# A hybrid encoder layer on one Trainium2 core: the row roots of the first norm reach all partitions by a store to DRAM and a broadcast load

## The reference

```
def rms_norm(x, g):
    y = xf * lax.rsqrt(jnp.mean(xf * xf, axis=-1, keepdims=True) + EPS)
    return (y * g)
h = rms_norm(x, mix_norm_g[l])
proj = h @ w_in[l]
u_a, v_a, q, k, v = jnp.split(proj, splits, axis=-1)
```

## Time and profile before

| what | value |
|---|---|
| median of 3 runs | 918.72 us (918.25 to 919.39) |
| the profiled execution | 919.09 us |
| its span | 917.3 us |
| PE busy | 909.7 us, 99% of the span |
| ACT, POOL, DVE busy | 429.6, 390.4, 588.9 us |
| granted TensorE clock | 0.999 of full speed |
| chain that ended last | PE 98%, issue 1% |

### The profile page before, as it was taken

The page is one execution under the profiler, slowest core; times in us unless marked ns, Lnnn a source line. Parts: engine busy times, 40 slices in busy tenths (PEclk is TensorE's granted clock), DMA queues, the critical chain, the costliest instruction groups (busy, mean ns, idle before and its releaser), DMA issues.

```text
span 917.3 us, 11969 instructions
## 1 busy us (share of the span) xinstructions
PE 909.7 (99%) x4229; PEld 750.0 (82%) x4229; DVE 588.9 (64%) x785; ACT 429.6 (47%) x835; POOL 390.4 (43%) x387
## 2 busy tenths in 40 slices
PE   9999999999999999999999999999999999999997
PEld 7888888787878888888888888888888888888885
DVE  5759879986779787464453653736547676544754
ACT  6747547856556543243333333333334454444451
POOL 1559732331244379557485574855754000000021
PEclk9999999999999999999999999999999999999999
DMA  9797453211242372744727437264366996656543
GB/s 330 235 267 232 115 161 105 80 70 70 92 138 88 97 220 69 232 136 134 228 68 233 138 126 227 76 226 146 121 223 248 372 368 192 201 187 203 185 138 138
DMA packets 151487, 158.56 MB, mean 173 GB/s; under 512 B 27576, under 2 KB 109060, under 8 KB 151428
## 3 DMA queue, kind: packets, MB, share of 16 engines
q1 hardware_dynamic: 150756, 157.40, 53.0%
q10 hardware_dynamic: 672, 0.40, 0.1%
HBM read 117.26 MB, written 40.50 MB: 172 GB/s over the span
## 4 chain that ended last, share of the span: by engine, by line
PE 98%; issue 1%; ACT 0%; POOL 0%; DVE 0%; POOLq 0%; ACTq 0%
PE ps L859 31%; PE ps L861 31%; PE ps L860 31%; PE ps L1031 1%; PE ps L1054 1%; PE ps L1043 1%; PE ps L979 1%; PE ps L1125 1%; PE ps L883 0%; PE ps L892 0%; PE ps L895 0%; PE ps L898 0%; PE ps L1000 0%; PE ps L990 0%; PE ps L1061 0%
## 5 line engine op out<-in xcount | busy, mean ns | idle before, releaser
L2116 DVE TENSOR_TENSOR P_lo<-P_raw,P_hi 128x512 fp32r<-128x512 f32 x132 | 119.5, 921 | 83.2 <-ACT P_hi L1554 78.8
L859 PE MATMUL ps<-T_hi,P_hi 128*128 128x512 f32 x352 | 136.9, 389 | 0.0
L860 PE MATMUL ps<-T_lo,P_hi 128*128 128x512 f32 x352 | 136.9, 389 | 0.0
L861 PE MATMUL ps<-T_hi,P_lo 128*128 128x512 f32 x352 | 136.9, 389 | 0.0
L801 POOL TENSOR_TENSOR wd<-wd 128x256 f32<-128x256 f32 x88 | 80.9, 919 | 93.6 <-DMA wd<-in_w_down 88.4
L859 PE MATMUL ps<-rb_hi,ra_hi 128*128 128x512 f32 x308 | 119.8, 389 | 0.0
L860 PE MATMUL ps<-rb_lo,ra_hi 128*128 128x512 f32 x308 | 119.8, 389 | 0.0
L861 PE MATMUL ps<-rb_hi,ra_lo 128*128 128x512 f32 x308 | 119.8, 389 | 0.0
L1668 ACT ACTIVATE ra_hi<-ra 128x512 fp32r<-128x512 f32 x77 | 48.6, 631 | 98.8 <-DMA rb<-w_down_T 61.0
L649 POOL TENSOR_SCALAR late<-late 128x1 f32<-128x1 f32 x12 | 6.0, 503 | 191.7 <-ACT junk L1736 178.1
L2225 DVE TENSOR_TENSOR ra_lo<-ra,ra_hi 128x512 fp32r<-128x512 f32 x77 | 55.7, 723 | 36.4 <-ACT ra_hi L1668 36.0
(11 more groups left out here) (286 smaller groups left out, 2018.0 us busy)
## 6 DMA issues: line engine op xcount, KB each, us to landing
wd<-in_w_down SPq DMA_DIRECT2D x44, 256.0 KB, 3.3
w_down_T<-wd SPq DMA_DIRECT2D x22, 512.0 KB, 5.0
ra<-act_S SPq DMA_DIRECT2D x44, 256.0 KB, 2.7
rb<-w_down_T SPq DMA_DIRECT2D x44, 256.0 KB, 3.0
act_S<-Q SPq DMA_DIRECT2D x33, 256.0 KB, 3.7
ra<-act_A SPq DMA_DIRECT2D x33, 256.0 KB, 4.4
rb<-in_w_down SPq DMA_DIRECT2D x33, 256.0 KB, 5.0
P_raw<-in_w_gate SPq DMA_DIRECT2D x22, 256.0 KB, 3.7
```

The source lines that it names most:

```text
L859: mm(dst, lhs[0], rhs[0], start=start, stop=False, skip_group_check=onto)
L860: mm(dst, lhs[0], rhs[1], start=False, stop=False, skip_group_check=onto)
L861: return mm(dst, lhs[1], rhs[0], start=False, stop=stop, skip_group_check=onto)
L2116: tt(w_l[p, m][:], src[:], w_h[p, m][:].bitcast(F32), ALU.subtract).then_inc(w_split, 1)
```

## The change

PE's eight transposes and ACT's two copies go. SP stores the roots as they lie (4 columns of 128 partitions) to a DRAM tensor in row order, two DMAs of 512 single elements each, waits for both, and loads each half back as one row of 512 broadcast to 128 partitions. `x_roots(1)` moves on POOL from behind the last bias copy to behind the 22nd of 29 (`ROOTS1_AT`), since SP now waits for it ahead of the bias wait. `evict` waits for both loads. Product P1_2 and P1_3, which waited for the copies because of their PSUM banks, now wait for the v_a results that lay there.

```
+    root_dram = nc.dram_tensor("row_roots", [T, P], F32, kind="Internal")
...
             for i in range(4):
                 in_block(wA_raw[i], i, 0, 0, slot_in[i])
+            for h in range(2):
+                sp.wait_ge(x_rstd, h + 1)
+                sp.dma_start(root_dram.ap()[HT * h:HT * h + HT].rearrange("t p -> p t"), rstd_x[:, HT * h:HT * h + HT], allow_slow_non_contiguous=True).then_inc(roots_out, 16)
+            sp.wait_ge(roots_out, 32)
+            for h in range(2):
+                sp.dma_start(roots[h][:], root_dram.ap()[HT * h:HT * h + HT].rearrange("t p -> (t p)").partition_broadcast(P)).then_inc(roots_in, 16)
             sp.wait_ge(bias_out, 16)
...
+            ROOTS1_AT = 3 * len(runs) // 4
...
+                if n == ROOTS1_AT:
+                    x_roots(1)
             last.then_inc(rel_built, 1)
-            x_roots(1)
...
-            def roots_T(h):
-                pe.wait_ge(x_rstd, h + 1)
-                pe.wait_ge(v_ready, HT * h + 3 + h)
-                for t in range(HT):
-                    r = HT * h + t
-                    last = nc.tensor.transpose(ps[:, ROOT_BANK[h], t * P:(t + 1) * P], rstd_x[:, r:r + 1].to_broadcast([P, P]), ident[:])
-                last.then_inc(rstd_T, 1)
...
-                    roots_T(0)
...
-                        pe.wait_ge(roots_ready, i - 1)
+                        pe.wait_ge(v_ready, (3, T)[i - 2])
...
-                if j == 0:
-                    roots_T(1)
...
-            def roots_copy(h):
-                act_e.wait_ge(rstd_T, h + 1)
-                if h:
-                    act_e.wait_ge(setup_T, 1)
-                actv(roots[h][:], ps[:, ROOT_BANK[h], :], ACT.Copy).then_inc(roots_ready, 1)
-
-            roots_copy(0)
...
-            roots_copy(1)
...
-                dve.wait_ge(roots_ready, half + 1)
+                dve.wait_ge(roots_in, 32)
```

More of the change, by code:

```diff
@@ L297, in hybrid_trunk_layer @@
     WARM = 15
-    ROOT_BANK, MIX_BANK = (2, 7), (3, 4)
+    MIX_BANK = (3, 4)
     STORES = [[slice(0, D)]] * (T - 1) + [[slice(0, C), slice(C, D)]]
@@ L317, in hybrid_trunk_layer @@
         x_in = [sem(f"x_in{s}") for s in range(4)]
-        x_sq, x_mse, x_rstd, rstd_T, roots_ready, hT0_hi_ready, hT_hi_ready, hT_ready = (
-            sem(n) for n in ("x_sq", "x_mse", "x_rstd", "rstd_T", "roots_ready", "hT0_hi_ready", "hT_hi_ready", "hT_ready"))
+        x_sq, x_mse, x_rstd, roots_out, roots_in, hT0_hi_ready, hT_hi_ready, hT_ready = (
+            sem(n) for n in ("x_sq", "x_mse", "x_rstd", "roots_out", "roots_in", "hT0_hi_ready", "hT_hi_ready", "hT_ready"))
         block_in = [sem(f"block_in{k}") for k in range(K)]
```

## The result

| | before | after |
|---|---|---|
| median of the runs, us | 918.49 (4 runs, 917.96 to 919.39) | 928.84 (4 runs, 928.03 to 929.79) |
| profiled execution, us | 919.09 | 929.79 |
| its span, us | 917.3 | 928.0 |
| mean granted clock of TensorE | 0.999 | 0.993 |

The ratio is 1.0111, with an interval of 1.0099 to 1.0123: the kernel is slower by 10.3 us, where +1.2 was forecast. 928.84 lies outside the range of 918.2 to 922.6, and beyond the upper end of the unknown cost as well (924.4). The sign of the forecast was right, its size was wrong by a factor of nearly nine.

A forecast was written before the change was run, and what follows sets the result against it. PE, busy in 99% of the span, was taken as the bound. Removing 0.88 us of PE work and adding 2.06 of idling gave +1.18, so 918.72 became 919.9 us, with an 8-in-10 range of 918.2 to 922.6.

The forecast's parts named there:

- the unknown cost: SP's wait for the root stores: landing time no row showed; at its upper end the kernel takes 924.4 us.
- roots at DVE: DVE first needs the roots at 57.16 us; loads land by about 54.2, leaving 3 us of room.
- less 0.46: At P1_1's first matmul: it comes later by SP's delay less 0.46 us.
- I take 49.3: Root stores on SP: out at 49.3 us, landing in 4.5 us like the bias store.
- That upper end, 9.0: Root stores' landing: each of 1024 elements costs as much as one bias store piece, 2 x 4.5 = 9.0 us.
- The bias store's landing: ACT's bias table store: issued 1.28 us later, still landing in 4.5 us, in at 49.9.
- SP's delay to PE: `s2` starts 1.64 us later; this passes through xb, D1, D2 and ACT, making P1_1 1.18 us later.
- rival C: Roots also late for `evict(0)` if stores take over 7 us, changing the time little further; chance 0.38 together with B.
- the 1.18: Delay of `evict(3)` and P1_1 in us, which nothing behind P1_1 adds to or gives back.
- B: At SP's wait: slow element stores, landing beyond 4.5 us costing one for one, 922.4 to 924.4; chance 0.38 with C.
- A: SP little delayed, both stores landing in 2.4 us; 0.45 us gained, 918.3; chance 0.13 with nearby cases.
- D: DVE's low parts run faster beside a shifted POOL, P1_1 on time; up to -0.88 us, 917.8; chance 0.04.

The follow-up runs named there:

- e3: Kernel before with second roots moved earlier on POOL and two root stores nobody waits for, elements 512 bytes apart in DRAM; 918.65 us.
- e2: Kernel before with second roots moved earlier on POOL and the change's two dense root stores added, nobody waiting for them, transposes kept; 926.60 us, ratio 1.0093.
- e5: Changed kernel with ACT's store of the bias table issued only after both root stores have landed; 930.42 us.
- e11: Changed kernel with the first half's root store and load moved to SP's idle stretch, at 30.67 us; 929.54 us.
- x1: As e2, but a single dense store of 128 elements, within 512 adjacent bytes, in place of two of 512; 926.01 us.
- e9: Changed kernel with root store elements 512 bytes apart and broadcast loads reading the norm's gains and offsets instead of the roots; 921.41 us, ratio 1.0030.
- x3: As e2, but the stored elements lie 8 bytes apart in DRAM; 922.56 us.
- e10: As e2, but the stored elements lie 16 bytes apart in DRAM; 920.56 us.
- e13: Changed kernel without root stores or their wait, gains and offsets loaded early instead of roots, second roots back behind POOL's copies; 917.80 us, ratio 0.9991.
- e4: As e2, but the roots stored as SBUF has them, 128 pieces of 16 bytes per store, still dense; 919.26 us.
- e6: Changed kernel with roots gathered by eight DMAs of 128 elements into one SBUF partition and broadcast from there, no DRAM; 940.84 us, ratio 1.0244.
- e12: Changed kernel, roots gathered into an SBUF row, stored contiguously to DRAM, broadcast; first half early, second via ACT, second roots behind POOL's copies; 921.27 us, ratio 1.0031.

## Why the prediction was wrong, step by step

The frame held. Place by place, forecast and measured:

| step | forecast | measured |
|---|---|---|
| second roots done on POOL | 43.8 | 43.46 |
| bias store issued | 45.4 | 44.72 |
| root stores issued | 44.25, 44.8 | 43.47, 44.0 |
| second root store's landing | 4.5 (2.4 to 9.0) | 12.65 |
| bias store's landing | 4.5 | 12.1 |
| `s2` starts | 50.3 | 57.54 |
| roots at DVE | 3 us of room | 5.6 late |
| first D2 high part | 69.6 | 77.59 |
| `evict(3)` starts | 76.9 | 83.92 |
| P1_1 against SP's delay | less 0.46 | 8.88 and 8.21, less 0.67 |

The issues on POOL, ACT and SP came within 0.8 us of the forecast, all a little early, as the execution was. **What failed is one sentence: "I take 49.3: it is the nearest row, a store to DRAM out of SBUF."** The nearest row by kind and by number of pieces was the bias store with its 512 pieces; but each of those is 764 bytes long (382 KB by 512), so that no short stretch gets many writes, and the question was what happens to pieces that lie side by side. The store took 12.65. The spacing accounts for most of it: the slower of the two stores took 4.2 at 512 bytes (e3) and 10.0 dense (e2), nobody waiting for either. The rest is not assigned; dense stores differ by as much between kernels (8.4 in e5, 10.7 and 11.0 in e11). The step was also wrong in kind: I bounded the stores' time as a sum over elements, and e11 and x1 show that half or an eighth of the elements costs the same. That upper end, 9.0, was a guess about the wrong quantity, and the truth lay outside it.

**The bias store's landing** I left at 4.5 with new traffic beside it. It was worth as much attention as the root stores: in e2 it alone sets SP's start, and PE waits 4.8 us for it. The prediction took the two stores as independent: each had its own 4.5, and SP went on at the later.

**SP's delay to PE** went down the forecast path, and its size came out partly by luck. P1_1 is late by SP's delay less 0.67 (8.88 to 8.21) and less 0.69 in e9 (2.96 to 2.27), against 0.46 forecast. But two steps within differ and nearly cancel. The prediction let the delay pass unchanged to the first D2 high part; it grew by 0.71, from 8.88 to 9.59 (68.00 to 77.59), and the last two `s2` issues, which took 2.04 us instead of 1.06, are in it: the first D load was issued 9.92 later (51.83 to 61.75). And it took the four low parts as a block of 6.67 us; they took 5.75, because they follow each high part as it comes, which gave 0.92 back. e9 shows the same two (3.55 at the high part, 2.26 at `evict(3)`). With the measured start of `s2` the prediction's own chain gives 918.49 + 8.88 - 0.46 = 926.9.

**The roots late** (rival C) came true beyond 7 us, as it said, and cost PE 0.97 us on a path where its idling partly replaces the transposes' time.

**What was left out** is the clock. That behind P1_1 "PE never idles for long", so that "nothing adds to the 1.18", looked for waits and not for what a wait does afterwards. With the 8.7 us of idling the granted clock was 0.50 from 79.5 until after 89 us, and that made 2.36 us more, a term that the prediction put at nothing. With it the chain makes 926.9 + 2.36 = 929.3; measured 928.84. In e9 the same happened after 3.1 us of idling, in x3 after 2.0. In e10, with 1.5 us, and in e3, with 0.2, the granted clock stayed at 1.00 there.

**Rivals.** B was the right mechanism (time to landing beyond 4.5 us one for one, at SP's wait), sized at 922.4 to 924.4. A's gain is 0.65 us where the cost is removed altogether (e13), and not clear of nothing. D fell: P1_1 wasn't on time, though its premise held in part, since the low parts took 0.92 us less.

**The prediction's own sums.** Three are a little off, and none matters for the outcome (0.48 is an issue of 0.43 and its gap). In A the root loads would be issued by 47.2 + 2 x 0.48 = 48.2, not 48.7. A landing of 7 us gives 922.4 under B and is written as 922.6 in the range. And the chances of the four cases add up to 1.00 already, which leaves no 0.02 for what isn't seen.

Here the Trainium skill, "DMA: Bandwidth & Descriptors", deserves the weight I didn't give it. It says that a non-contiguous last dimension becomes a descriptor for each element and should be rearranged, and that below 512 B a transfer is done by read-modify-write. Laid beside the runs: one descriptor per element costs little by itself (e3, 3.9 us at the median for 512), and pieces of 16 bytes, far below 512 B as well, landed in 3.1 to 3.8 (e4). A read-modify-write would fit writes that queue up for the same stretch, but no run separates it from another reason to go in turn. The rule pointed to the upper end; the measurements go beyond it.

**What stays open.** That dense writes go one after the other is a reading that fits the landings; no record shows it. The idle engines of e11 speak for a place behind the engines, and against one within them; a dense store in which each stretch is written by one engine only would tell more, and was not run. How long the stretch is. Why e4's dense pieces of 16 bytes are quick. Why the spread store took up to 5.9 us in e9 and up to 4.2 in e3. And why the bias store is caught in it when it comes behind the elements.

## What to carry to other kernels

Before you trade an engine's work for a small store to DRAM, look at where the elements land: single elements side by side took 6 to 13 us whatever their number; spread by 64 bytes or more, or in pieces of 16 bytes, 3 to 6. Price the transfer by what it does to others as well: the store that was waited for anyway went from 4.5 to 12.1 us. And ask first what the removed work is worth at the place where PE and its feeder meet: here the whole gain was 0.65 us, at most 1.7 by its interval, so there was little to pay with.

## What the runs showed of the hardware that I had not expected

- 128 single elements of 4 bytes into 512 adjacent bytes of DRAM took 9.8 us (x1); 512 dense ones in one store took 10.7 and 11.0 (e11); two such stores at once took 6.4 to 12.65 (after, e2, e5); two with the elements 512 bytes apart took 3.5 to 4.2 (e3), and up to 5.9 in e9.
- For the last 4 and 5 us before such a store landed, the DMA engines moved nothing that shows (e11, share 0.00).
- With the bias table's store behind the dense elements, the DMA engines count as 85% busy at 18 to 24 GB/s, nearly all of it on the table's queue (81.5% of 48 to 52 us). A high share isn't bandwidth: read the two columns together.
- A gather of 128 single elements into one SBUF partition landed in 3.0 us at the median of eight (e6), though SP waited 6.1 us for four of them in e12; a broadcast of 2 KB out of one partition to 128 took 11.7 and 20.3 us, from DRAM 3.7.
- TensorE stopped at 76.07 us, was granted 0.50 of its clock from about 79.5, and still ran at that for about 5 us after it had work again: 2.36 us on top of a wait of 8.7. In x3 a wait of 2.0 us was followed by 3.4 us at 0.50, in e10 one of 1.5 by none.
